# The expert sum of a PEER layer, moved from whole 128x128 diagonals to 32x32 diagonals in the sixteen parts of the TensorE array

## The reference

```python
def peer_ffn(xn, w_query, sub_keys, peer_u, peer_v):
    ...
    idx = jnp.take_along_axis(cand_i, best_pos, axis=-1)      # 128 experts for each token
    gate = jax.nn.softmax(best_s, axis=-1)
    ...
        h = jnp.einsum('thkd,td->thk', peer_u[ib], xb).astype(jnp.float32)
        a = (gb * jax.nn.gelu(h, approximate=False)).astype(xb.dtype)
        return jnp.einsum('thk,thkd->td', a, peer_v[ib])      # the expert sum
...
    x = x + y @ w_out
    x = x + peer_ffn(rms_norm(x, norm2_g), w_query, sub_keys, peer_u, peer_v)
```

## Time and profile before

| | |
|---|---|
| three runs | 3075.08 us median (3071.18 to 3080.69) |
| the profiled execution | span 3067.0 us from first to last instruction |
| PE matmul busy | 2694.1 us (88%), 8608 records |
| DVE busy | 2135.5 us (70%) |
| ACT busy | 1193.2 us (39%) |
| POOL busy | 1260.2 us (41%) |
| moved by DMA | 1170.33 MB, 382 GB/s over the span |

### The profile page before, as it was taken

One profiled execution on the slowest core, in us unless ns is written; L12 is line 12 of the kernel. 1 busy time (PEld: TensorE's weight loads), 2 busy tenths in 40 slices (PEclk: granted clock), 3 DMA queues, 4 the chain that ended last, 5 costly groups with the idle time before them and its releaser, 6 DMA issues.

```text
span 3067.0 us, 29307 instructions
## 1 busy us (share of the span) xinstructions
PE 2694.1 (88%) x8608; PEld 1481.6 (48%) x8608; DVE 2135.5 (70%) x5243; ACT 1193.2 (39%) x3444; POOL 1260.2 (41%) x1028
## 2 busy tenths in 40 slices
PE   7869899989998999788998999888999877877777
PEld 6656465445654555345554555435555332333333
DVE  4555577976657778866656778876756777776765
ACT  3322445753324545533223545653323323232232
POOL 0023343344334454444444444334444555445443
PEclk9789999999999999899999999989999999889989
DMA  4269999999999999999999999989999999999998
GB/s 160 67 255 414 368 397 394 378 354 401 398 420 415 407 419 417 361 358 404 413 415 420 397 378 421 393 331 368 412 420 421 420 418 422 405 420 417 418 416 353
DMA packets 173808, 1170.33 MB, mean 382 GB/s; under 512 B 19280, under 2 KB 19408, under 8 KB 42576
## 3 DMA queue, kind: packets, MB, share of 16 engines
q0 software_dynamic: 147456, 1073.81, 86.0%
q1 hardware_dynamic: 26192, 94.65, 8.1%
HBM read 1166.28 MB, written 2.10 MB: 381 GB/s over the span
## 4 chain that ended last, share of the span: by engine, by line
PE 43%; DMA 22%; DVE 20%; ACT 8%; issue 5%; POOL 2%; SPq 0%; DVEq 0%; ACTq 0%
PE ysum L543 29%; DMA gather<-experts,idx 22%; DVE gather L1028 10%; PE bank L404 9%; DVE sd L811 3%; PE bank L505 3%; ACT diag L750 2%; POOL gather L362 2%; ACT amp L742 2%; ACT L592 1%; PE bank L451 1%; PE bank L419 1%; ACT gel L735 1%; DVE shared L838 1%; ACT sd L592 1%
## 5 line engine op out<-in xcount | busy, mean ns | idle before, releaser
L543 PE MATMUL ysum<-gather,diag 128*128 128x512 f32 x4096 | 1920.7, 624 | 300.1 <-ACT diag L750 298.6
L362 POOL DMA_INDIRECT gather<-experts,idx x1024 | 1260.0, 1230 | 1785.1 <-PE ysum L543 1519.9
L1028 DVE CUSTOM_DVE_ANT_0 gather<-gather,xc 128x1024 f32<-128x1024 f32 x1024 | 1222.8, 1224 | 545.3 <-DMA gather<-experts,idx 543.0
L543 PEld LDWEIGHTS ysum<-gather,diag 128*128 128x128 f32 x4096 | 802.5, 200 | 1320.2 <-issue 926.5
L735 ACT ACTIVATE gel<-hdot 128x4 f32<-128x4 f32 x255 | 52.4, 205 | 1519.2 <-DVE hdot L1028 1501.7
L404 PE MATMUL bank<-xnT,w 128*128 128x256 f32 x1984 | 457.2, 385 | 7.4 <-DVE xnT L800 7.4
L404 PEld LDWEIGHTS bank<-xnT,w 128*128 128x128 f32 x1984 | 376.6, 192 | 86.0 <-issue 29.9
L750 ACT ACTIVATE diag<-cc,amp 128x128 f32<-128x128 f32 x1020 | 326.8, 387 | 35.8 <-PE ysum L543 35.0
L742 ACT ACTIVATE amp<-gel,gate 128x1 f32<-128x1 f32 x1020 | 216.9, 283 | 8.3
L811 DVE RECIPROCAL sd<-sd 128x256 f32<-128x256 f32 x60 | 105.1, 1751 | 128.5 <-ACT sd L592 128.3
L735 ACT ACT_TABLE_LOAD x124 | 159.1, 1283 | 2.2
(11 more groups left out here) (116 smaller groups left out, 1495.2 us busy)
## 6 DMA issues: line engine op xcount, KB each, us to landing
w<-weights SPq DMA_DIRECT2D x168, 512.0 KB
gather<-experts,idx POOLq DMA_INDIRECT x1024
y_out<-x SPq DMA_DIRECT2D x4, 512.0 KB, 8.0
x<-x_in SPq DMA_DIRECT2D x2, 512.0 KB, 5.3
g2b<-g_rows SPq DMA_DIRECT2D x2, 512.0 KB
x<-x_in SPq DMA_DIRECT2D x1, 1024.0 KB, 12.0
cc<-consts_in SPq DMA_DIRECT2D x1, 603.5 KB, 6.6
late<-late_in SPq DMA_DIRECT2D x2, 256.0 KB, 9.9
```

The source lines that it names most:

```text
L362: pool.indirect_dma_start(gather[:, n % SLOTS, :], None, uv_d[m // 2], bass.IndirectOffsetOnAxis(ap=idx[:, g % 2, k:k + 1], axis=0)).then_ ...
L543: mm = nc.tensor.matmul(ysum[:, hf * 512:(hf + 1) * 512], diag[:, n % NDIAG, :], gather[:, n % SLOTS, DM + hf * 512:DM + (hf + 1) * 512], ...
L1028: e = V.tensor_tensor_reduce(out=gather[:, n % SLOTS, 0:DM], in0=gather[:, n % SLOTS, 0:DM], in1=xc[:, :], scale=1.0, scalar=0.0, op0=ALU. ...
```

## The change

The 128x128 diagonal is cut to its four 32x32 blocks. `diag` becomes 128x32: in each group of 32 partitions stands the diagonal of those 32 tokens, written by ACT from a new constant (four 32x32 identities below each other). PE multiplies each 32x32 block q with the 32 partitions of the slot, for each half `hf` of the channels, so that a step is eight matmuls of 32 rows, 32 columns of weights and 512 moving columns in place of two. The rows of the array follow from the token group q; the columns from the half and from whether n is even or odd. The result of token group q goes to its own PSUM bank, in the 32 partitions `2*(n % 2) + hf`. `ysum` is therefore four banks, with even and odd steps summed apart, and `add_tile` becomes 16 additions of 32x512 that also move the partitions. The mixers keep four banks in place of six.

```diff
-CC_N = CC_EPS + 1
+QUAD = 32
+PARTS = P // QUAD
+CC_N = CC_ID64 + QUAD
...
-BANKS = 6
+BANKS = 4
...
-        diag = sb("diag", NDIAG, P)
+        diag = sb("diag", NDIAG, QUAD)
...
-        ysum = ctx.enter_context(nc.psum_tensor("ysum", [P, DM], f32))
+        ysum = ctx.enter_context(nc.psum_tensor("ysum", [P, PARTS * 512], f32))
...
+        ident64 = cc[:, CC_ID64:CC_ID64 + QUAD]
...
                 for hf in range(2):
-                    mm = nc.tensor.matmul(ysum[:, hf * 512:(hf + 1) * 512], diag[:, n % NDIAG, :],
-                                          gather[:, n % SLOTS, DM + hf * 512:DM + (hf + 1) * 512],
-                                          start=k == 0, stop=k == HEADS * TOPK - 1)
+                    for q in range(PARTS):
+
+                        toks, outs = (slice(QUAD * i, QUAD * (i + 1)) for i in (q, 2 * (n % 2) + hf))
+                        mm = nc.tensor.matmul(ysum[outs, q * 512:(q + 1) * 512], diag[toks, n % NDIAG, :],
+                                              gather[toks, n % SLOTS, DM + hf * 512:DM + (hf + 1) * 512],
+                                              start=k < 2, stop=k >= HEADS * TOPK - 2)
                 mm.then_inc(s_yc, 1)
...
-                nc.scalar.activation(diag[:, n % NDIAG, :], ident, ACT.Copy, scale=amp[:, c % 2, j:j + 1]).then_inc(s_dg, 1)
+                nc.scalar.activation(diag[:, n % NDIAG, :], ident64, ACT.Copy, scale=amp[:, c % 2, j:j + 1]).then_inc(s_dg, 1)
...
-                V.tensor_tensor(x[:, t, :], ysum[:, :], x[:, t, :], ALU.add).then_inc(s_x, 1)
+                for odd in range(2):
+                    for q in range(PARTS):
+                        for hf in range(2):
+                            toks, outs = (slice(QUAD * i, QUAD * (i + 1)) for i in (q, 2 * odd + hf))
+                            part = x[toks, t, hf * 512:(hf + 1) * 512]
+                            e = V.tensor_tensor(part, ysum[outs, q * 512:(q + 1) * 512], part, ALU.add)
+                            if odd and hf and q == PARTS - 1:
+                                e.then_inc(s_x, 1)
+                            elif hf and q == PARTS - 1:
+                                chain(dve, e)
```

More of the change, by code:

```diff
@@ L58 @@
 SP_N = SP_LAM + 128
-CC_ID, CC_O64, CC_O32, CC_DB, CC_DD, CC_IOTA, CC_INVW, CC_CORR, CC_SLI, CC_EPS = (
-    0, 128, 256, 384, 640, 1152, 1168, 1170, 1202, 1206)
-CC_N = CC_EPS + 1
+CC_ID, CC_O64, CC_O32, CC_DB, CC_DD, CC_IOTA, CC_INVW, CC_CORR, CC_SLI, CC_EPS, CC_ID64 = (
+    0, 128, 256, 384, 640, 1152, 1168, 1170, 1202, 1206, 1207)
+QUAD = 32
+PARTS = P // QUAD
+CC_N = CC_ID64 + QUAD
 def slope(h):
@@ L1145, in layout_consts @@
     c[:, CC_EPS] = EPS
+    c[:, CC_ID64:CC_ID64 + QUAD] = q % QUAD == np.arange(QUAD)[None]
     return c
```

## The result

| | before | after |
|---|---|---|
| median of four runs | 3074.67 us (3071.18 to 3080.69) | 3122.01 us (3119.2 to 3129.02) |
| ratio, 95% interval | | 1.0157 (1.014 to 1.0175) |
| profiled execution, span | 3067.0 us | 3119.3 us (its own time 3121.14) |
| granted TensorE clock, mean | 0.948 | 0.745 |

The account below looks back on a forecast made before the run. Transfers were the floor in full stages, PE set the pace in two others, and a DVE-ACT ping-pong the rest. Gains 24 + 17 + 8 = 49, losses 13 + 26 + 5 + 4 = 48: 3075 us, range 3032 to 3128.

Parts of the forecast that it names:

- the tail's 3.5 us of PE: At the kernel's end, PE's last sums finish 3.5 us earlier, against an addition 8.8 us longer.
- The additions: DVE's sixteen additions at eight tile ends, 10.0 us for 1.22: losses of 13, 26 and, at the end, 8.8 us.
- four tile ends fall into full stages: At chunks 64, 128, 192, 224, slots in flight hide most of the additions; 3.3 us lost each, 13 in all.
- The banks: Mixers with four banks: jobs wait for their own group's bank, nine of them projections; 4 us lost, bounds 0 and 33.
- most stand in stages with full DMA queues or behind a late PE: Nine projections that wait for a bank are mostly hidden, so only 4 us are lost.
- slower by the banks: Rival: each of the nine projections is exposed, and the sums behind them; 29 us more, 3104 us, chance 0.09.
- PE's step: Expert sum on PE: two passes, 0.86 us a step in place of 1.78, 3.5 us a chunk for 7.1.
- rival of 3119 us: Column parts don't overlap or passes can't be issued faster; a step stays at 1.7 us; chance 0.20.
- Of the 32 us I take 24: From 190 to 590 and 1690 to 1940 us, a faster PE falls under the transfers and recovers 24 us.
- The ping-pong stages: 590 to 700, 1237 to 1345, 1940 to 2110 us: PE's shorter sum gains 17 us, ACT's shorter diagonal 8.
- The diagonal's 8: ACT's diagonal of 32 columns saves 0.3 us a chunk, counting only in the DVE-ACT loop: 8 us, bounds 0 and 13.
- The clock: PE's granted clock falls under 0.9 from 2412 us on without harm, but stays at 1 beside the mixers.

Follow-up runs that it names:

- e6: Kernel before with four mixer banks, sixteen additions per tile and two sets of sum banks in turn, so PE does not stop for them: 3163.51 us.
- e1: Kernel before with four mixer banks in place of six, nothing else: 3095.29 us, ratio 1.0087.
- e3: Changed kernel with one addition of 128x1024 per tile in place of sixteen, leaving out the rest of the sum: 3053.06 us, ratio 0.995.
- e10: e6 with the additions in the middle of each block spread four at a time behind four chunks: 3150.48 us, ratio 1.0243.
- e13: Kernel before with four mixer banks and eight additions of 32x512 per tile in place of one of 128x1024: 3125.47 us, ratio 1.0172.
- e4: Changed kernel with eight of the sixteen parts, two sum banks, three additions per tile and six mixer banks; computes the whole sum: 3034.46 us, ratio 0.9895.
- e8: e4 with five mixer banks in place of six: 3034.28 us, ratio 0.9884.
- e11: e8 with two unused float32 matmuls of 128x512 into a spare bank behind each chunk's sums: 3042.89 us, ratio 0.9902.
- e7: e4 with ACT writing the whole 128x128 diagonal again, of which PE uses the four blocks: 3041.91 us, ratio 0.9912.

## Why the prediction was wrong

The forecast was a balance of 49 us of gains and 48 of losses. Measured, with the tail's 3.5 us of PE among the gains: 42 for 52.5, against 95 for 52. The time lies inside the range of 3032 to 3128 us, but that is no merit of the forecast's mechanism: the range was wide enough to take in the rivals. Three terms failed by about the same amount: the banks by 22 us, the additions by 21 (16 by the ratios), and the gain where PE set the pace by 17.

**The additions: 69 us (64 by the ratios), forecast 48 (13 + 26, and 8.8 at the end).** That sixteen take 10 us was near (11.2, and 10.44 in e6), and so were the sizes in the ping-pong stages (forecast 8.8 each; e6 over e1 at the tile ends: 9.3, 9.3 and 9.0) and at the end (6.5, forecast 5). What failed is the step "four tile ends fall into full stages ... 1.6 to 4 us of empty queue each, I take 3.3". Against before these ends are 11.6, 8.5, 8.4 and 8.8 us longer, 37 for 13 (2 to 3 us of the first are the banks'). Some of that is made good in the chunks that follow: up to the next end, against e3, it is 5.5, 9.1, 6.8 and 6.5, 28 for 13. The step counted from PE's stop alone. It named the key search and the next dot products as queued behind the additions but gave them no price: 3.9 us of search and 4.6 us of dot products with the 1.2 of the addition were already nearly a full chunk. e6, e10 and e13 show it: taking PE's stop away brings nothing, spreading the additions brings some, and half of them cost at most half. That the slots hide a part was right in kind: in the last two stages they hid 3 to 3.6 of the 4.0 us of e13.

**The banks: 26 us, forecast 4.** The step "most stand in stages with full DMA queues or behind a late PE" failed. The jobs and their waits were found beforehand, and the upper bound of 33 us was near. But chunks 66 to 89 were full (414 GB/s) and yet had PE 96% busy: a full queue isn't slack when the engine behind it has none. The 5.6 us in the mixer ahead of everything, where nothing hides a wait, were not counted at all. With the shorter sum chunks 66 to 89 lose 12 us in place of 19 (e3). In the kernel after they are only 7.8 us longer than before, behind a tile end (63 to 66) that is 11.6 longer. The rival "slower by the banks" had the mechanism and its size, 29 us, at a chance of 0.09.

**PE's step: 0.86 us forecast, 0.61 measured at the higher level** (2.43/4), 1.04 at the lower. The side of the argument was right, and the rival of 3119 us, whose number comes nearest, was wrong in its cause: the column parts do overlap. The forecast's two passes a step are what e4 shows, where all steps use the same parts: 3.66/4 = 0.91 us. In the kernel after even and odd steps also run beside each other. The Trainium skill, "TensorE: Matmul & The Clock Gate", Part 3, has matmuls strictly first in, first out ("pc-monotone in start AND end"). The prediction took this for eight pairs nearly one behind another, about 3.4 us a step, and this trace shows 0.61. What fails is that reading: the rule is about the order of starts and ends, and the same section has matmuls in different parts of the array overlap. The ends in this profile are modelled, so no run here tests their order. The 10.6 times of that section, which the prediction also used, is near what came: 64 x 0.43 / 2.43 = 11.3.

**Where PE set the pace: 24 us forecast, about 7 came.** "Of the 32 us I take 24" failed: e3 against e1 gives 7 us for chunks 0 to 30 and 130 to 150 together, and e8 against before, without the fourth bank's loss, 8. PE's busy share fell from 92% to 67% and the rate of transfers did not rise. The chain of work that ended last, from 200 to 560 us, was 55% PE before (34.9% the sum, 20.4% the projection) and is 17% PE and 38% transfers after: PE did leave the path, but the transfers stood close behind it. The rows before already had a sign of this. The DMA share in the two stages was 0.98 and 0.99 where 1.01 means no rest, so that only about 17 of the 32 us (an estimate: 400 x 0.03/1.01 + 250 x 0.02/1.01) were idle time of the DMA engines; the rest was a lower rate with the engines busy, which a faster PE need not change. Why the rate is lower there is left open; in e8 PE is 75% busy there at 397 GB/s, and the clock is one more candidate that e11 doesn't exclude.

**The ping-pong stages: 17 + 8 us forecast, 22 measured** (e3 against e1 for chunks 30 to 42, 89 to 98, 150 to 164: 7.2, 1.2 and 13.7). The diagonal's 8 is e7's 7 in size, but only about half of it comes in these stages, where the prediction had all of it. The sum is right, its split only in part.

The rest of the 42 us is 7 in chunks 66 to 89, 3.5 at the end, and pieces of under 3.

**The clock** fell beside the mixers too (0.62 to 0.81 by stage), which the prediction had named as a thing that would make it wrong. It isn't the cause of the slowdown: e4 and e3 have clocks of 0.842 and 0.763 and are faster than the kernel before. What the clock takes from the gains is not shown.

The profiled execution after lies 1.8 us above its span, not 8.1: what the prediction put around the span is mostly the difference between executions (each execution on record is 1.8 to 1.9 us over its own span).

## What to carry to other kernels

Before an operation is lengthened, add up what its engine already does between the two deadlines around it, what is queued behind it included. Here 0.3 of 10 us were left; the nine slots hid most of 4 us more in the stages without a mixer, and less than half of nine or ten. A resource that is taken from a neighbour (here two PSUM banks) is to be priced where that neighbour's engine is busiest, not where the queues are fullest. And a layout that saves an engine off the path may be had more cheaply: with half of the parts, two banks and three additions, the same idea is 35 us faster than the kernel before rather than 47 slower.

## What was not expected of the hardware

- Float32 matmuls of 32x32 parts, two passes each, overlap across all sixteen parts and across steps: 64 passes in 2.43 us, where one pass lasts 0.43. With eight parts in use the same 64 take 3.66 us.
- Four row parts can write one bank at the same time when each writes partitions of its own (e4), at no loss that these runs show.
- DVE's additions of 32x512 take 686 ns, operations of 128x512 693: a quarter of the partitions costs a full instruction.
- PE's granted clock was 0.61 from 2412 us on, with PE idle for 6 us between chunks of 4 us; the same chunk takes 4.16 us at the level of 1.2 GHz and 2.43 us at 2.4 GHz.
